# Layer 0's expert call: one token tile's pair weights through GpSimd scatter-adds, and one-hot products for two tiles instead of three

## The chip, the core and the metric

The kernel runs on one core of a Trainium2 chip. The metric is the device time of one execution in microseconds (us); the time quoted for a kernel is the median of its runs. One execution was also taken by the hardware profiler, and all rows below are from that one.

## What is computed

Two layers of attention-like mixers over 256 latent and 256 context tokens, each followed by a PEER expert block, and then a second block of layers. Only the expert block of layer 0 matters here. It works on 512 tokens of width 1024, in four tiles of 128 tokens:

```python
q = (hb @ wq).reshape(tc, PEER_HEADS, 2, PEER_HALF)
s = einsum('thpk,hpnk->thpn', q, keys)            # 8 heads, 2 x 128 keys
s_top, i_top = top_k(s, 16)
cand = s_top[:, :, 0, :, None] + s_top[:, :, 1, None, :]
best, pos = top_k(cand, 16)                       # 16 pairs (i, j) of each head: 128 pairs a token
g = softmax(best)
act = gelu(einsum('td,thed->the', hb, u[eid]))    # eid = 128 * i + j
out = einsum('the,thed->td', g * act, v[eid])
```

There are 128 x 128 = 16384 experts. A token uses at most 128 of them.

## The kernel before

Three of the four tiles (0, 1, 2; together 384 tokens) are computed densely: all 16384 experts are multiplied with all 384 tokens, and a table of weights, zero almost everywhere, picks what counts. The fourth tile (number 3, `SPARSE`) is computed by gathering: for each of its 128 pairs a token, GpSimd fetches the 128 rows of u (`L3484`) and of v (`L3490`), and VectorE makes a dot product (`L3027`) and later a weighted sum (`L3048`).

The dense part has two halves of 128 rounds. A round of the first half ("up") is one block of 128 experts, read from `peer_u` by SyncE's DMA. ScalarE rounds the block to the high part (`L3283`), VectorE makes the low part (`L2925`), both three rounds ahead of use. TensorE multiplies both with the hidden states in 24 products of 384 columns (`L3178` to `L3180`), and ScalarE applies the gelu (`L3290`). A round of the second half ("down") does the same with `peer_v` and the weighted activations (`L3217`). Twelve early up rounds (3, 5, 8, ... 30) also carry a piece of the next layer's modulation.

Beside the up rounds VectorE finds the pairs of each tile ("select"), in the order `TILES = (0, 3, 1, 2)`. How far it goes in a round is a budget in estimated ns: `EARLY_NS` up to the round before the tables begin, then `TABLE_NS` until all four tiles are selected. After this the gathered tile's pieces follow, `PICKS_NS` a round in the up half and `DOWN_NS` a round in the down half; a piece is counted as 1250. The budgets are written into VectorE's program when it is built; they wait for nothing. Within select, ScalarE takes the exponent of the shifted scores (`L3351`, `exp_ready`); its place in ScalarE's queue is the round in which VectorE is planned to have the shifted scores ready (`L2953`), and everything behind it in ScalarE's queue waits with it. The gate of each 8 dot products (`L3323`) stands in ScalarE's queue in the same manner.

A dense tile's pairs are turned by TensorE into `pair_table`: for each token (a column) its 128 values of i, of j and of the share. The table of pair weights then comes four tokens at a time, a group: VectorE compares i and j with 0..127 (`L3058`), ScalarE scales the second by the share (`L3297`, four instructions), TensorE multiplies the two for each token (`L3203`, 8 records for four products), and ScalarE copies the 128 x 512 result (`L3306`). Each four groups SyncE stores a block of 16 tokens, 1 MB, to the DRAM tensor `pair_weights` (`L3469`). 384 tokens are 96 groups and 24 blocks. `TABLE_ROUND` says in which round TensorE does a group, after the 24 products of that round: one group in each round from 32 on, and two in the twelve even rounds 60 to 82, so that the last is in round 115.

GpSimd does nothing in this stage but the gathers: three fetches of u at once, as soon as the spots, the modulation and the first table are ready, then each waits for the dot product that frees its slot. The down half begins by loading the first weights from `pair_weights`.

## Time and profile before

| what | us |
|---|---|
| median of 3 runs (lowest, highest) | 3693.56 (3688.54, 3696.64) |
| the profiled execution, its own time | 3688.0 |
| its span in the trace | 3686.2 |
| up rounds, first to last product | 485.7 to 1175 |
| down rounds | 1183.2 to 1713.5 |
| TensorE busy, share of the span | 3516.4 (95%) |

TensorE is busy for 95% of the span, so what matters is which products it has to do and where it waits. A round is recognised by its 24 products of 384 columns; dividing a stretch by its number of rounds gives the price of a kind of round.

### The profile page before, as it was taken

The numbers are of one execution on the slowest core, as the hardware profiler recorded it, in microseconds if no ns is written. First come the engines' busy times: TensorE is split into PE (matmuls) and PEld (weight loads), VectorE is DVE, ScalarE is ACT, GpSimd is POOL, SyncE is SP. The second block draws the span as 40 slices with busy tenths as digits, with TensorE's granted clock in tenths as the row PEclk, the third lists the DMA queues.
The fourth block names the chain that finished last, engine by engine and source line by source line (L and its number), as shares of the span: only waits on it lengthen the run. The fifth ranks groups of instructions, "written<-read, shape, count | busy, mean of one in ns | idle before, by whom it ended". The sixth has DMA issues, their size and how long they took to land. (4 is left out here: it accounts for less than half of the span.)

```text
span 3686.2 us, 56123 instructions
## 1 busy us (share of the span) xinstructions
PE 3516.4 (95%) x21807; PEld 3143.1 (85%) x21807; DVE 2731.1 (74%) x5467; ACT 1690.3 (46%) x3033; POOL 348.6 (9%) x274
## 2 busy tenths in 40 slices
PE   7999999989999999998999999999997899989899
PEld 6777998989998888887778999988886889988798
DVE  4557379988885888887546987778887677767775
ACT  4343333556663333334543444443334545564554
POOL 0000000014443333330000000000000000000000
PEclk9999999999999999999999999999998999999999
DMA  5133357569998999995124765556664214432143
GB/s 229 71 115 137 138 194 300 173 224 340 371 375 296 333 391 370 377 357 186 56 86 156 233 220 172 169 197 243 242 245 165 98 63 169 186 142 109 69 183 137
DMA packets 184072, 766.75 MB, mean 208 GB/s; under 512 B 23360, under 2 KB 70976, under 8 KB 133888
## 3 DMA queue, kind: packets, MB, share of 16 engines
q1 hardware_dynamic: 146944, 628.92, 47.3%
q0 software_dynamic: 36864, 134.23, 9.4%
q8 instruction: 175, 2.87, 0.3%
q14 instruction: 89, 0.73, 0.1%
HBM read 696.24 MB, written 66.85 MB: 207 GB/s over the span
## 5 line engine op out<-in xcount | busy, mean ns | idle before, releaser
L2925 DVE TENSOR_TENSOR expert_ring_low<-expert_ring,expert_high 128x1024 fp32r<-128x1024 f32 x256 | 312.9, 1222 | 143.5 <-ACT expert_high L3283 137.2
L3283 ACT ACTIVATE expert_high<-expert_ring 128x1024 fp32r<-128x1024 f32 x256 | 270.6, 1057 | 276.2 <-PE ps L3217 264.0
L2192 ACT ACTIVATE expert_high<-expert_ring 128x1024 fp32r<-128x1024 f32 x256 | 270.6, 1057 | 211.3 <-PE ps L2119 211.3
L1922 DVE TENSOR_TENSOR expert_ring_low<-expert_ring,expert_high 128x1024 fp32r<-128x1024 f32 x256 | 311.6, 1219 | 70.7 <-ACT expert_high L2192 70.7
L3178 PE MATMUL ps<-hidden_high,expert_high 128*128 128x384 f32 x1024 | 352.6, 344 | 0.0
L3179 PE MATMUL ps<-hidden_low,expert_high 128*128 128x384 f32 x1024 | 344.4, 336 | 0.0
L3180 PE MATMUL ps<-hidden_high,expert_ring_low 128*128 128x384 f32 x1024 | 344.0, 336 | 0.0
L2088 PE MATMUL ps<-peer_hT_high_peer,expert_high 128*128 128x256 f32 x1024 | 293.9, 287 | 0.6 <-DVE expert_ring_low L1922 0.5
L2089 PE MATMUL ps<-peer_hT_low,expert_high 128*128 128x256 f32 x1024 | 287.0, 280 | 0.0
L2090 PE MATMUL ps<-peer_hT_high_peer,expert_ring_low 128*128 128x256 f32 x1024 | 287.0, 280 | 0.0
L3484 POOL DMA_INDIRECT x<-in_peer_rows,spots x128 | 171.1, 1336 | 971.0 <-ACT mod_next L2378 558.8
L3217 PE MATMUL ps<-expert_high,weighted_high 128*128 128x512 f32 x768 | 237.7, 391 | 9.4 <-DVE weighted_low L3098 9.4
L3217 PE MATMUL ps<-expert_ring_low,weighted_high 128*128 128x512 f32 x768 | 237.0, 390 | 0.0
L3217 PE MATMUL ps<-expert_high,weighted_low 128*128 128x512 f32 x768 | 237.0, 390 | 0.0
L5596 PE MATMUL ps<-hT_high,units_high 128*128 128x256 f32 x704 | 200.2, 284 | 0.0
L5596 PE MATMUL ps<-hT_low,units_high 128*128 128x256 f32 x704 | 199.5, 283 | 0.0
L5596 PE MATMUL ps<-hT_high,weight_ring_low 128*128 128x256 f32 x704 | 199.4, 283 | 0.0
L3490 POOL DMA_INDIRECT chosen_v<-in_peer_v,spots x128 | 171.1, 1336 | 263.2 <-DVE x L3048 246.9
L2088 PEld LDWEIGHTS ps<-peer_hT_high_peer,expert_high 128*128 128x128 f32 x1024 | 194.4, 190 | 1.2 <-DVE expert_ring_low L1922 1.2
L219 DVE TENSOR_TENSOR weight_ring_low<-weight_ring,units_high 128x1024 fp32r<-128x1024 f32 (+1 forms) x148 | 166.9, 1189 | 38.3 <-ACT units_high L210 38.1
L3178 PEld LDWEIGHTS ps<-hidden_high,expert_high 128*128 128x128 f32 x1024 | 194.1, 190 | 0.8 <-issue 0.8
L2089 PEld LDWEIGHTS ps<-peer_hT_low,expert_high 128*128 128x128 f32 x1024 | 194.7, 190 | 0.0
(790 smaller groups left out, 9616.4 us busy)
## 6 DMA issues: line engine op xcount, KB each, us to landing
expert_ring<-in_peer_u SPq DMA_DIRECT2D x128, 1024.0 KB
expert_ring<-in_peer_v SPq DMA_DIRECT2D x128, 1024.0 KB
weight_ring<-in_ffn_w_up SPq DMA_DIRECT2D x22, 2048.0 KB, 7.3
weight_ring<-in_w_in SPq DMA_DIRECT2D x14, 2048.0 KB, 7.8
weight_ring<-in_w_mod SPq DMA_DIRECT2D x12, 2048.0 KB, 8.6
mod_slot<-in_w_mod SPq DMA_DIRECT2D x12, 2048.0 KB, 10.4
pair_weights<-pair_weights_out SPq DMA_DIRECT2D x24, 1024.0 KB
pair_weights_in<-pair_weights SPq DMA_DIRECT2D x15, 1536.0 KB, 15.6
```

Source lines behind the costliest of these rows:

```text
L1922: dve.tensor_tensor(piece(low, n), piece(raw, n), high[:, n % LEAD, :].bitcast(F32), ALU.subtract).then_inc(low_done, 1)
L2088: pe.matmul(o, b[:, s], hT_h[:, c, :], start=(c == 0), stop=False)
L2089: pe.matmul(o, b[:, s], hT_l[:, c, :], start=False, stop=False)
L2090: mm = pe.matmul(o, lo[:, s], hT_h[:, c, :], start=False, stop=(c == DC - 1))
L2192: act.activation(high[:, n % LEAD, :], piece(raw, n), ACT.Identity).then_inc(high_done, 1)
L2925: dve.tensor_tensor(self.piece(G.e_low, n), self.piece(G.e_raw, n), G.e_high[:, n % LEAD, :].bitcast(F32), ALU.subtract).then_inc(self.S.l ...
L3178: pe.matmul(o, b[:, s], B.hs[0][:, c, 0:DW], start=(c == 0), stop=False)
L3179: pe.matmul(o, b[:, s], B.hs[1][:, c, 0:DW], start=False, stop=False)
L3180: mm = pe.matmul(o, lo[:, s], B.hs[0][:, c, 0:DW], start=False, stop=(c == DC - 1))
L3217: mm = pe.matmul(G.ps[:, 2 * t + h, :], (B.ah, B.al)[x][:, r % 3, t * P:(t + 1) * P], v[y][:, h * 512:(h + 1) * 512], start=(r == 0 and (x ...
L3283: act.activation(G.e_high[:, n % LEAD, :], self.piece(G.e_raw, n), ACT.Identity).then_inc(S.high_done, 1)
L5596: mm = pe.matmul(G.ps[:, k % 8, 0:SEQ], w[x][:, c, q * P:(q + 1) * P], self.hT[y][:, c, :], start=(c == 0 and (x, y) == PASSES[0]), stop=( ...
```

## The change

The first tile (0, now `STREWN`) leaves the one-hot products. Its places in `pair_weights` are computed by VectorE (`own_spots`), and GpSimd adds its shares there: 128 indirect DMAs with `compute_op=ADD`, each of 128 single numbers. The eight blocks of this tile are cleared beforehand by eight copies of 1 MB from a constant of zeros, issued by SyncE in the mixer stage long before. Since two heads of a token can have the same pair, GpSimd waits after each 16 scatters (one head) until they have landed. The first 96 scatters come before the first gather; the other 32 are woven with the gathers, one behind each.

The one-hot products are left for 256 tokens, 64 groups and 16 blocks: one group a round in rounds 48 to 111, none doubled. The budgets change. The first fetches of u now wait for the table of tile 1, since tile 0 has none.

```diff
-TABLES_AT = 32
-TABLES = DW // TOKS
+TABLES_AT = 48
+TABLES = (DW - P) // TOKS
-EARLY_NS, TABLE_NS, PICKS_NS, DOWN_NS = 3900, 3300, 2200, 1450
+EARLY_NS, TABLE_NS, PICKS_NS, DOWN_NS = 3200, 3000, 2300, 1500
-DOUBLED = range(60, 84, 2)
-TABLE_ROUND = [r for r in range(TABLES_AT, N_KEYS) for _ in range(2 if r in DOUBLED else 1)][0:TABLES]
+STREWN = 0
+STREWN_FIRST = 6 * PEER_TOPK
+OWN_BLOCKS = P // BLOCK
+TABLE_ROUND = range(TABLES_AT, TABLES_AT + TABLES)
@@ the mixer stage, SyncE
                     ws.run_ahead(sp, u0 + 6)
+                    for b in range(OWN_BLOCKS):
+                        sp.dma_start(G.w_dram[b], G.d["zeros"]).then_inc(G.cleared, 16)
                     sp.wait_ge(S.roped, 6)
@@ select, VectorE
+            elif tile == STREWN:
+                dve.wait_ge(S.base_landed, 16)
+                dve.tensor_scalar(B.own_spots[:, :], B.where[:, :], float(BLOCK), B.base[:, 0:1], ALU.mult,
+                                  ALU.add).then_inc(S.own_ready, 1)
@@ SyncE, before the down half's first weights are loaded
-                sp.wait_ge(S.table_ready, DT)
+                sp.wait_ge(S.table_ready, DT - 1)
+                sp.wait_ge(G.strewn, 16 * PAIRS)
@@ GpSimd
+    def strew(self, pool, m):
+        G, B = self.G, self.B
+        places = G.w_dram.rearrange("b p (n o) -> (b p n) o", o=1)
+        if m and m % PEER_TOPK == 0:
+            pool.wait_ge(G.strewn, 16 * m)
+        pool.indirect_dma_start(places, bass.IndirectOffsetOnAxis(B.own_spots[:, m:m + 1], 0), B.own_share[:, m:m + 1],
+                                None, compute_op=ALU.add).then_inc(G.strewn, 16)
 
     def run(self, pool):
         G, S, B = self.G, self.S, self.B
+        pool.wait_ge(G.cleared, 16 * OWN_BLOCKS)
+        pool.wait_ge(S.own_ready, 2)
+        for m in range(STREWN_FIRST):
+            self.strew(pool, m)
         pool.wait_ge(S.spots_ready, 1)
         pool.wait_ge(S.mod_out, 1)
         pool.wait_ge(S.table_ready, 1)
...
+            if STREWN_FIRST + n < PAIRS:
+                self.strew(pool, STREWN_FIRST + n)
```

On TensorE, the end of round 60 before, where two groups of products (x8 as the program counts them) stand behind the round's last products:

```order
L3179 MATMUL ps<-hidden_low_3340,expert_high 128x384
L3180 MATMUL ps<-hidden_high_3339,expert_ring_low 128x384
L3203 MATMUL ps<-hot_weighted_4886,equal_4885 128x128 x8
L3178 MATMUL ps<-hidden_high_3339,expert_high 128x384
L3179 MATMUL ps<-hidden_low_3340,expert_high 128x384
```

The same place now:

```order
L3189 MATMUL ps<-hidden_low_3348,expert_high 128x384
L3190 MATMUL ps<-hidden_high_3347,expert_ring_low 128x384
L3213 MATMUL ps<-hot_weighted_4894,equal_4893 128x128 x4
L3188 MATMUL ps<-hidden_high_3347,expert_high 128x384
L3189 MATMUL ps<-hidden_low_3348,expert_high 128x384
```

One group is left there. Over the whole program the rows with x8 (12 of them) are gone, and of the 72 with x4 64 are left.

On VectorE, before, the round in which the last tile's shifted scores (`best_shift`) are made, with the comparison of a group (`equal`) ahead; this is planned for round 48:

```order
L2925 TENSOR_TENSOR expert_ring_low<-expert_ring,expert_high 128x1024
L3058 TENSOR_TENSOR equal_4885<-iota,pair_table_4911 128x1024
L1754 MAX_INDEX best_pos_4897<-best_4896,top_work_4891 128x8 x4
L2953 TENSOR_TENSOR best_shift_4903<-best_4896 128x128
L2957 TENSOR_SCALAR pos_row_4898<-best_pos_4897 128x128
L2958 CAST pos_f_4899<-best_pos_4897 128x128
L2961 CAST pos_f_4899<-pos_row_4898 128x128
L2964 TENSOR_SCALAR pos_ij_4900<-pos_f_4899 128x128
L2967 SCALAR_TENSOR_TENSOR pos_f_4899<-pos_ij_4900 128x128
L2970 SCALAR_TENSOR_TENSOR pos_ij_4900<-pos_f_4899 128x128
L2974 TENSOR_TENSOR one_hot_4901<-pos_ij_4900,iota 128x2048
L2925 TENSOR_TENSOR expert_ring_low<-expert_ring,expert_high 128x1024
```

The same place now, planned for round 54:

```order
L2929 TENSOR_TENSOR expert_ring_low<-expert_ring,expert_high 128x1024
L3068 TENSOR_TENSOR equal_4893<-iota,pair_table_4919 128x1024
L1752 MAX best_4904<-top_work_4899 128x8 x4
L1756 MAX_INDEX best_pos_4905<-best_4904,top_work_4899 128x8 x4
L2957 TENSOR_TENSOR best_shift_4911<-best_4904 128x128
L2961 TENSOR_SCALAR pos_row_4906<-best_pos_4905 128x128
L2962 CAST pos_f_4907<-best_pos_4905 128x128
L2965 CAST pos_f_4907<-pos_row_4906 128x128
L2968 TENSOR_SCALAR pos_ij_4908<-pos_f_4907 128x128
L2971 SCALAR_TENSOR_TENSOR pos_f_4907<-pos_ij_4908 128x128
L2929 TENSOR_TENSOR expert_ring_low<-expert_ring,expert_high 128x1024
```

A round holds less of select than before, and the comparison stands in it as before. Select as a whole ends in round 61 instead of 54, and the eighth dot product of the gathered tile, which the first gate waits for, is planned for round 65 instead of 58.

On GpSimd, before, the stage's queue from its start (the first ten fetches of u, then u and v in turn):

```order
L3601 UNCONDITIONAL_BRANCH
L3484 DMA x<-in_peer_rows,spots_4913 128x1024 x10
L3490 DMA chosen_v_4882<-in_peer_v,spots_4913 128x1024
L3484 DMA x<-in_peer_rows,spots_4913 128x1024
L3490 DMA chosen_v_4882<-in_peer_v,spots_4913 128x1024
```

Now, first the start and then, behind the dots, the place where v begins:

```order
L3630 UNCONDITIONAL_BRANCH
L3492 DMA pair_weights<-own_shares_4921,own_spots_4920 6291456x1 x96
L3508 DMA x<-in_peer_rows,spots_4923 128x1024
L3492 DMA pair_weights<-own_shares_4921,own_spots_4920 6291456x1
...
L3508 DMA x<-in_peer_rows,spots_4923 128x1024
L3514 DMA chosen_v_4890<-in_peer_v,spots_4923 128x1024
L3492 DMA pair_weights<-own_shares_4921,own_spots_4920 6291456x1
L3508 DMA x<-in_peer_rows,spots_4923 128x1024
```

96 scatters stand ahead of the first fetch, and one behind each of the first 32 fetches of u.

## Rows read from the trace of the kernel before

**Rows 1.** The page: span and busy time, and the two DMA queues that carry data

```profile
span 3686.2 us, 56123 instructions
PE 3516.4 (95%) x21807; PEld 3143.1 (85%) x21807; DVE 2731.1 (74%) x5467; ACT 1690.3 (46%) x3033; POOL 348.6 (9%) x274
...
q0 software_dynamic: 36864, 134.23, 9.4%
```

**Rows 2.** Windows: stretch and length, then busy us (count) by engine, clock, DMA share, GB/s

```profile
485.70:658.80 173.10, 173.10 (x1096) 153.06 (x1095) 153.79 (x597) 60.44 (x85) 2.56 (x2) 1.00 0.71 261
658.80:1125.60 466.80, 447.79 (x2793) 443.79 (x2791) 409.48 (x645) 286.09 (x661) 160.24 (x111) 0.98 0.83 303
894.00:958.80 64.80, 62.58 (x403) 61.44 (x402) 55.40 (x60) 44.41 (x110) 29.32 (x20) 1.00 0.94 338
984.10:1125.60 141.50, 141.50 (x900) 141.50 (x898) 123.89 (x133) 86.75 (x200) 70.70 (x50) 1.00 0.98 377
1125.60:1171.50 45.90, 45.90 (x267) 45.90 (x267) 24.21 (x25) 16.19 (x23) 15.87 (x11) 1.00 0.80 308
...
1183.20:1713.50 530.30, 528.31 (x2336) 437.15 (x2336) 452.74 (x601) 198.62 (x271) 163.44 (x133) 1.00 0.95 348
```

**Rows 3.** Waits of TensorE between 658.8 and 1125.6: total us, times, longest

```profile
PE ps L3203 <- ACT hot_weighted L3297: 13.1, 6, 5.7
...
PE ps L3203 <- ACT pair_weights_out L3306: 5.7, 9, 2.5
```

**Rows 4.** Timeline around 757: start, duration, engine, line, what; idle before and releaser

```profile
750.99 1.22 DVE L2925 TENSOR_TENSOR expert_ring_low<-expert_ring,expert_high 128x1024 fp32r<-128x1024 f32 x1
...
757.30 1.21 DVE L2925 TENSOR_TENSOR expert_ring_low<-expert_ring,expert_high 128x1024 fp32r<-128x1024 f32 x1
...
760.76 0.29 DVE L2953 TENSOR_TENSOR best_shift<-best 128x128 f32<-128x128 f32 x1
...
761.09 0.31 ACT L3351 ACTIVATE best_exp<-best_shift 128x128 f32<-128x128 f32 x1 [5.13 <-DVE best_shift L2953]
...
765.06 2.04 PE L3203 MATMUL ps<-hot_weighted,equal 128*128 128x128 f32 x8 [5.67 <-ACT hot_weighted L3297]
```

**Rows 5.** Timeline of the first gathers and of the first gate

```profile
655.88 1.17 POOL L3484 DMA_INDIRECT x<-in_peer_rows,spots  x1 [558.80 <-ACT mod_next L2378]
...
795.53 1.68 POOL L3484 DMA_INDIRECT x<-in_peer_rows,spots  x1 [135.54 <-DVE x L3027]
...
803.89 1.89 POOL L3484 DMA_INDIRECT x<-in_peer_rows,spots  x1 [1.74 <-DVE x L3027]
...
816.65 1.22 DVE L3027 SCALAR_TENSOR_TENSOR x<-x,hidden_rows 128x1024 f32<-128x1024 f32 x1 [4.07 <-DMA x<-in_peer_rows,spots]
...
820.56 0.21 ACT L3323 ACTIVATE acts<-dots 128x8 f32<-128x8 f32 x1 [8.72 <-DVE x L3027]
```

**Rows 6.** Groups between 485.7 and 1176: busy us, mean ns, idle before and releasers

```profile
L3297 ACT ACTIVATE hot_weighted<-equal,pair_table 128x128 f32<-128x128 f32 x384 | 122.2, 391 | 64.5 <-DVE equal L3058 64.5
L3058 DVE TENSOR_TENSOR equal<-iota,pair_table 128x1024 f32<-128x1024 f32 x96 | 115.8, 1218 | 0.0
...
L3484 POOL DMA_INDIRECT x<-in_peer_rows,spots x66 | 96.4, 1461 | 794.7 <-ACT mod_next L2378 558.8 <-DVE x L3027 226.4 <-issue 9.5
```

**Rows 7.** The fetches of u by line (min/median/max ns), and the last share of tile 0

```profile
L3484 POOL DMA_INDIRECT x<-in_peer_rows,spots x128: 933/1019/1982, 655.9 to 1627.5; - x128
...
558.40 0.29 DVE L3001 TENSOR_TENSOR selected<-best_exp,best_sum 128x128 f32<-128x128 f32 x1
```

**Rows 8.** SyncE's queue in the mixer stage, first use of the mask, and traffic there

```profile
115.16 0.33 SPq L1693 DMA_DIRECT2D scan_mask<-in_scan_mask  x1
152.68 0.33 SPq L172 DMA_DIRECT2D weight_ring<-in_w_mod  x1
...
L1176 DVE SCALAR_TENSOR_TENSOR mlstm_d<-ps,gcol,scan_mask x32: 475/617/753, 244.8 to 305.5; 128x256 f32<-128x256 f32 x16, 128x512 f32<-128x512 f32 x16
...
112.00:152.00 40.00, 40.00 (x189) 28.09 (x188) 22.01 (x52) 17.12 (x35) 0.00 (x0) 1.00 0.22 86
```

More of the change, by code:

```diff
@@ L55 @@
 SCOPES = []
-STAGE_SEMS = 27
+STAGE_SEMS = 26
 BIG_SEMS = 88
@@ L97, in stage @@
         loads_landed = own[-1]
-        assert len(names) + (3 if beside is not None else 0) < len(own)
+        assert len(names) + (3 if beside is not None else 0) + (1 if loads else 0) <= len(own)
         @block.sync
@@ L2982, in select @@
                 yield 2200
-            if dense >= 2:
-                dve.wait_ge(S.sel_turned, dense - 1)
             for which in range(2):
@@ L2991, in select @@
             step(dve.tensor_reduce(B.sm[:, :, 0], B.ex[:, :, :], AX.X, ALU.add))
-            if tile == SPARSE:
+            if tile in (SPARSE, STREWN):
                 step(dve.scalar_tensor_tensor(B.where[:, :], sel[:, 0, :], float(N_KEYS), sel[:, 1, :], ALU.mult, ALU.add))
@@ L2997, in select @@
                 dve.tensor_copy(B.spots[:, :], B.where[:, :]).then_inc(S.spots_ready, 1)
+            elif tile == STREWN:
+                dve.wait_ge(S.base_landed, 16)
+                dve.tensor_scalar(B.own_spots[:, :], B.where[:, :], float(BLOCK), B.base[:, 0:1], ALU.mult,
+                                  ALU.add).then_inc(S.own_ready, 1)
             yield 600
             step.wait()
-            share = (B.share[:, :] if tile == SPARSE else sel[:, 2, :]).rearrange("p (h m) -> p h m", h=PEER_HEADS)
+            share = {SPARSE: B.share[:, :], STREWN: B.own_share[:, :]}.get(tile, sel[:, 2, :]).rearrange("p (h m) -> p h m", h=PEER_HEADS)
             mm = dve.tensor_tensor(share, B.ex[:, :, :], B.sm[:, :, 1:2].broadcast_to([P, PEER_HEADS, 16]), ALU.mult)
@@ L3003, in select @@
                 step(mm)
+                yield 300
+                continue
+            if tile == STREWN:
+                mm.then_inc(S.own_ready, 1)
                 yield 300
@@ L3058, in equal @@
         dve.tensor_tensor(B.eq[:, g % 2, :, :, :], G.iota[:, :].unsqueeze(1).unsqueeze(1).broadcast_to([P, 2, TOKS, P]),
-                          B.table[:, 0:2, g * TOKS:(g + 1) * TOKS].unsqueeze(3).broadcast_to([P, 2, TOKS, P]),
+                          B.table[:, 0:2, P + g * TOKS:P + (g + 1) * TOKS].unsqueeze(3).broadcast_to([P, 2, TOKS, P]),
                           ALU.is_equal).then_inc(S.eq_ready, 1)
@@ L3184, in turn_selected @@
         G, S, B = self.G, self.S, self.B
-        k = [n for n, t in enumerate(TILES) if t != SPARSE][d]
+        k = [n for n, t in enumerate(TILES) if t not in (SPARSE, STREWN)][d]
         pe.wait_ge(S.sel_ready, d + 1)
@@ L3250, in run @@
                 pe.wait_ge(S.score_s, SCORE_GROUPS // 2)
-            for d in range(DT):
+            for d in range(DT - 1):
                 if r == at[f"turn{d}"]:
@@ L3295, in shares @@
         for k in range(TOKS):
-            t = g * TOKS + k
+            t = P + g * TOKS + k
             act.activation(B.hot_w[:, g % 2, k, :], B.eq[:, g % 2, 1, k, :], ACT.Identity,
@@ L3405, in run @@
         G, S, B, mod = self.G, self.S, self.B, self.mod
+        sp.dma_start(B.base[:, :], G.d["pair_base"]).then_inc(S.base_landed, 16)
         mod.load(sp, 0, self.mod_landed)
@@ L3421, in run @@
                     mod.load(sp, u + 2, self.mod_landed)
-            while stored < BLOCKS and TABLE_ROUND[4 * stored + 3] + 2 <= UJ * p + 1:
+            while stored < BLOCKS - OWN_BLOCKS and TABLE_ROUND[4 * stored + 3] + 2 <= UJ * p + 1:
                 self.store_w(sp, stored)
@@ L3559, in first_experts @@
     B.ge_kept = room(96, 24).take("gelu_kept", [P, STAY - RING, DW], F32)
+    few = room(138, 1.8125)
     B.table = room(127.5, 4.5).take("pair_table", [P, 3, DW], F32)
+    B.own_spots = room(127.5, 0.5).take("own_spots", [P, PAIRS], U32)
+    B.own_share = room(129, 0.5).take("own_shares", [P, PAIRS], F32)
     B.ge_out = room(132, 6).take("gelu_out", [P, 4, DW], F32)
-    few = room(138, 1.8125)
     B.spots = few.take("spots", [P, PAIRS], U32)
@@ L3582, in first_experts @@
     F.ln_cols = few.take("ln_cols", [P, 2, DC], F32)
+    B.base = few.take("own_base", [P, 1], F32)
     B.x_last = F.x_last = room(28.25, 4).take("x_last", [P, D], F32)
@@ L5961, in make_shared @@
     G.v_landed = [nc.alloc_semaphore(f"chosen_v{s}_landed") for s in range(V_SLOTS)]
+    G.w_dram = nc.dram_tensor("pair_weights", [BLOCKS, P, N_KEYS * BLOCK], F32).ap()
+    G.cleared = nc.alloc_semaphore("pair_weights_cleared")
+    G.strewn = nc.alloc_semaphore("shares_strewn")
     G.e_turn = 0
@@ L6098, in constants @@
     f = np.float32
-    c = {"ident": np.eye(P, dtype=f), "pick": np.tile(np.eye(PAD, dtype=f)[:, 0:2], (P // PAD, 1)), "iota": np.tile(np.arange(P, dtype=f), (P, 1))}
+    p = np.arange(P)
+    base = (p // BLOCK * N_KEYS * N_KEYS * BLOCK + p % BLOCK).astype(f)[:, None]
+    c = {"zeros": np.zeros((P, N_KEYS * BLOCK), f), "pair_base": base, "ident": np.eye(P, dtype=f), "pick": np.tile(np.eye(PAD, dtype=f)[:, 0:2], (P // PAD, 1)), "iota": np.tile(np.arange(P, dtype=f), (P, 1))}
     m = np.full((P, 2, QK_WIDTH), NEG, f)
```

10 lines of the change are left out of this document (5 added, 5 removed).

## The prediction

> **What bounds the kernel now.** I read the page first: TensorE is busy for 95% of the span [rows 1], so time can be won only where its products get fewer or its waits shorter. Then the windows of the expert stage [rows 2], because every round has the same 24 products and a stretch divided by its rounds gives a price. Rounds without a group (116 to 126): 45.9 / 11 = 4.17 us. Rounds with one group (88 to 115): 141.5 / 28 = 5.05, so a group costs TensorE 0.88. Rounds 72 to 82 hold six doubled and five single ones: (64.8 - 5 x 5.05) / 6 = 6.59, so the second group of a round costs 1.54, not 0.88. In all three stretches TensorE has no idle time to speak of, and its clock was granted at 1.00, the level of 2.4 GHz.
>
> The whole stretch from round 32 to 115 took 466.8 us for 84 rounds and 12 doublings [rows 2]. By these prices it would be 84 x 5.05 + 12 x 1.54 = 442.7. The rest, 24.1, is stalls. The waits of TensorE there are almost all at the one-hot products: 13.1 us for ScalarE's scaled one-hots, 5.7 for its copies out [rows 3]. The timeline shows where the longest comes from [rows 4]: VectorE needs 757.30 - 750.99 = 6.3 us for a round that TensorE does in 5.05. It is late with the shifted scores, ScalarE stands 5.13 us at its exponent with the gelu, the next block and the one-hots queued behind it, and TensorE then waits 5.67. The second place is the first gate [rows 5]: the fetches issued at 803.89 and after are awaited by VectorE for 4.07 us at 816.65, so ScalarE stands 8.72 us at the gate and TensorE waits again.
>
> The down half is TensorE's alone: 530.3 us with 528.3 busy for 128 rounds, 4.14 a round [rows 2].
>
> **The change, part by part.** I count from 658.8 (round 32) to the end of round 127, before: 466.8 + 12 x 4.17 = 516.8 us.
>
> *TensorE's work.* After: 32 rounds without a group (32 to 47, 112 to 127), 64 with one: 32 x 4.17 + 64 x 5.05 = 456.6. That is 516.8 - 456.6 = 60.2 less if nothing stalled any more; of it 36.1 is work (20 fewer rounds with a group x 0.88 = 17.6, 12 doublings x 1.54 = 18.5) and 24.1 is all stalls of before. So the question is which stalls come back.
>
> *Start of the tables.* VectorE does two comparisons in the round before the first group, now round 47. I take 1 us of stall (0 to 2; one of the waits of [rows 3]).
>
> *Fourth exponent, now round 54.* Before, VectorE had table rounds from 32 on ahead of round 48, of 6.3 us at the worst [rows 4] and some 5.9 on average by the budget (3.3 of select plus two instructions of 1.14 net, and the small gaps). In the nine rounds since its last pause it fell behind by about 9 x (5.9 - 5.05) = 7.7 us. Now the budget is 0.3 less, and only seven table rounds stand before round 54: 7 x 0.55 = 3.9, plus 1.1 for the doubled comparison: 5.0. The stall there, about 9 us before with the slower clock after it (the 2.04 us group of [rows 4], against about 1.05 for an undisturbed one), becomes about 9 - 2.7 = 6.5. Bounds: 2 and 9.
>
> *Rounds 32 to 47.* They get shorter for TensorE (4.17), and VectorE with 3.2 of select and one low part is at 4.4 to 4.5: no longer slack as in the modulation rounds (173.1 / 32 = 5.4 each [rows 2]). The third exponent (round 38) and the first turning (44) fall here. ScalarE and VectorE work three rounds ahead, which hides most of it. I take 4 us, bounds 0 and 8.
>
> *First gate, now round 65.* The same start of gathers, with 1.84 dot products a round instead of 1.76 and a scatter between two fetches. I take the stall of before, about 6.5 with its waits of [rows 5], plus 1.5 for one scatter ahead of the late fetch: 8. Bounds 4 and 14.
>
> *Doubled rounds and the block stores.* The copies out that waited (5.7 [rows 3]) belong to them; one group a round leaves eight rounds for two blocks. 0 to 1: I take 0.5, with the second turning.
>
> Sum of stalls: 1 + 6.5 + 4 + 8 + 0.5 = 20. After: 456.6 + 20 = 476.6, against 516.8: **40 us less**.
>
> *VectorE and ScalarE* lose 32 comparisons of 1.22 and 128 scalings of 0.39 [rows 6]; they are not the bound in those rounds, and what this gives is counted above.
>
> *GpSimd's scatters.* No row shows an accumulating DMA. Nearest: a fetch of u, 0.93 to 1.98 us, median 1.02 over the stage, mean 1.46 in the busy up half [rows 6, 7], plus 0.3 from one to the next. I take 1.34, so 1.64 each. Tile 0's shares were ready at 558.4 [rows 7]; with the lower budget some two rounds later, about 570. The 96 take 157 us. The five waits are for a landing: nothing below, and above the 12.8 us from 803.89 to 816.65 [rows 5]; I take 4. End: 570 + 157 + 20 = 747 (697 to 853 with both ends everywhere: 96 x 1.32, or 96 x 2.28 and 64 us of waits). The first dot product comes at about 658.8 + 16 x 4.17 + 4 + 13 x 5.05 + 1 + 6.5 = 803. So 56 us of cover; the three first fetches are issued after the table of tile 1 instead of at 655.88, and are not missed before 803. If the cover is gone, each us is TensorE's: behind the dot product stand the low parts of all further blocks.
>
> The Trainium skill ("DMA: Bandwidth & Descriptors", section "Anatomy of one DMA") gives a fixed cost of about 2.0 us to a DMA from GpSimd. If that held the queue for each scatter, it would be 96 x 2.3 = 221 us, an end at about 811 and an 8 us loss; the fetches of u here, at a median of 1.02 us, hold GpSimd's queue for less.
>
> *The woven 32.* A pair then costs GpSimd 3 x 1.76 = 5.3 us in the busy half, against one pair in 5.05 / 0.92 = 5.5. Just enough; 0, up to 10 if a scatter takes 2.
>
> *Their transfers.* 36864 packets of the gathers' queue took 9.4% of 16 engines [rows 1]: 0.094 x 16 x 3686 / 36864 = 0.15 us a packet of 4 KB. 128 packets of one number: 1.2 us at most of the 16 engines if they cost as much, nothing at the least; I take 0.2. With one group a round the DMA share was 0.98 at 377 GB/s and TensorE did not wait [rows 2]; the picks add 0.04 pairs of 1 MB a round, 8 GB/s. 0, up to 15.
>
> *Clearing.* 8 MB at about 113 us, behind SyncE's last load and ahead of the mask (115.16). The DMA share is 0.22 there [rows 8]. At 377 GB/s it is 22 us, at half that 45: over at about 160. The mask is first used at 244.8, the next load (152.68) later than that. SyncE's eight issues take some 4 us in which it had nothing to do. 0 on the path.
>
> *Down half.* 1500 instead of 1450: VectorE stays at about 3.6 of 4.14 us. It ends with products, unchanged: 0.
>
> The sum stands against the profiled execution: 3688.0 - 40 = 3648. The median of runs lies 5.6 above it; I say **3651**, between the two ways of placing it.
>
> **Rivals.**
> 1. *Slow scatters: slower than before.* Three things of the list above in one mechanism: GpSimd's queue is serial, and the first fetch stands behind 96 scatters. At a price s each (with the gap), the fetches come at 590 + 96 s, and the loss is 96 s - 213, plus 23 (s - 2.0) for the woven ones once v is fetched too. It eats 40 us at s = 2.5. At s = 3.3 the time would be 3688 - 40 + 104 + 30 = 3782. For it: an accumulate has to read before it writes, 128 places each in another row of the memory, and 16 are outstanding at a time where the gathers had three or four. Against: the longest fetch, 512 KB, took 1.98. The skill's same page (section "Specifications") says that transfers under 512 B are done as read-modify-write, which speaks for it; no row here can show what that costs.
> 2. *DMA becomes the bound in rounds 62 to 120.* At 0.98 share and 5.05 a round, a scatter at 1.2 us of all engines would make 5.05 x 0.98 + 0.1 + 1.2 = 6.2 for the 32 rounds or so in which they are woven: half of it late, about 20 us lost: 3670.
> 3. *The stalls are not there.* With smaller budgets VectorE is never late, and the exponent and gate wait cost nothing: 60 instead of 40, 3631.
> 4. *TensorE's groups were hidden anyway*, so that nothing is gained: 3690. Against: no idle time in the stretches of [rows 2].
>
> **How the numbers follow.** What a measurement can tell here is 0.2%, 7.4 us. Chances: forecast, 25 to 52 us less, 0.62; rival 2 and late first fetches, 8 to 25 less, 0.16; rival 3, more than 52, 0.05; within 7.4, 0.05; slower, 0.12. Faster 0.83, same 0.05, slower 0.12. The range: the stall bounds sum to 6 and 32, so 26 to 54 below 3688 to 3693; I leave out rival 1 and half of rival 2: 3637 to 3674.
>
> **What would show it.** A single-group round at 5.05 and an empty one at 4.17; the up half (485.7 to 1175) ending near 1135; the down half still 530. No wait at copies out. ScalarE waiting at the exponent of round 54 and the gate of 65, some 5 us each. Scatters at about 1.3 us on GpSimd, ended before 800. Wrong if scatters take over 2.4, if VectorE waits long at the first dot product, if rounds 62 to 95 are over 5.2, or if the down half grows.

## The result, and the profile after

The changed kernel takes 3673.99 us (median of 4 runs, 3669.64 to 3674.43) against 3693.48 (3688.54 to 3696.64): ratio 0.9946, interval 0.9929 to 0.9963. It is faster, by 19.5 us, just under half of the 40 that were forecast. The profiled execution has a span of 3672.4 against 3686.2.

The page of the changed kernel, the lines that answer to [rows 1]:

```profile
span 3672.4 us, 55502 instructions
...
PE 3492.1 (95%) x21548; PEld 3116.7 (85%) x21548; DVE 2695.5 (73%) x5436; ACT 1638.2 (45%) x2873; POOL 591.6 (16%) x402
...
q0 software_dynamic: 55296, 134.31, 10.6%
```

TensorE's busy time is 24 us less. GpSimd's went from 348.6 to 591.6; the scatters are 249.4. The gathers' queue has 18432 packets more, 144 a scatter (128 with a number each and 16 more, all of 4 bytes), and only 0.1 MB more.

The windows of the changed kernel (columns as in [rows 2]): rounds 0 to 31; 32 to the first dot products; to round 91; nearly 13 rounds with one group; the down half:

```profile
488.20:661.00 172.80, 172.80 (x1093) 152.71 (x1093) 140.61 (x514) 60.66 (x85) 70.64 (x40) 1.00 0.78 260
661.00:826.00 165.00, 156.94 (x932) 155.39 (x931) 148.32 (x432) 80.20 (x154) 123.97 (x67) 0.98 0.68 180
826.00:985.60 159.60, 142.22 (x855) 141.03 (x855) 120.17 (x135) 81.79 (x187) 131.57 (x80) 0.95 0.95 328
1014.00:1079.00 65.00, 65.00 (x414) 65.00 (x413) 58.55 (x64) 40.34 (x93) 34.80 (x25) 1.00 1.01 396
...
1165.00:1696.20 531.20, 527.47 (x2332) 436.36 (x2333) 461.87 (x613) 198.68 (x271) 176.07 (x141) 1.00 0.97 355
```

The fourth row has no idle TensorE, and rounds there take 5.05 us: the price of a round was right. The third row is where the loss is: TensorE idles for 17.4 of 159.6 us, and GpSimd is busy for 131.6; with the 0.30 us that stand between any two of its 80 instructions, 24 us, hardly anything is left. The down half is unchanged (531.2 against 530.3).

The waits of the changed kernel between rounds 32 and 127: what waited, for what, total, times, longest. They answer to [rows 3]:

```profile
DVE x L3037 <- DMA x<-in_peer_rows,spots: 43.3, 16, 8.5
...
ACT acts L3333 <- DVE x L3037: 35.8, 7, 12.6
...
PE ps L3213 <- ACT hot_weighted L3307: 23.8, 7, 8.5
...
POOL pair_weights L3492 <- DMA pair_weights<-own_shares,own_spots: 14.9, 4, 5.9
...
ACT best_exp L3361 <- DVE best_shift L2957: 8.9, 2, 5.1
```

The first three lines are a chain. VectorE waits for a fetched u 16 times; ScalarE stands at the gate for VectorE's dot product with the one-hots queued behind; TensorE then waits for the scaled one-hots. The wait for the copies out [rows 3] is gone, and the exponent's is as long as before (5.1).

The changed kernel's timeline, where GpSimd runs through three pairs, and the first gate with TensorE's wait for it:

```profile
847.50 0.21 ACT L3333 ACTIVATE acts<-dots 128x8 f32<-128x8 f32 x1 [12.56 <-DVE x L3037]
...
849.47 0.77 PE L3213 MATMUL ps<-hot_weighted,equal 128*128 128x128 f32 x2 [8.53 <-ACT hot_weighted L3307]
...
865.79 2.69 POOL L3492 DMA_INDIRECT pair_weights<-own_shares,own_spots  x1 [0.30 <-issue]
868.78 0.97 POOL L3508 DMA_INDIRECT x<-in_peer_rows,spots  x1 [0.30 <-issue]
870.06 0.95 POOL L3514 DMA_INDIRECT chosen_v<-in_peer_v,spots  x1 [0.30 <-issue]
871.32 2.04 POOL L3492 DMA_INDIRECT pair_weights<-own_shares,own_spots  x1 [0.30 <-issue]
873.67 1.39 POOL L3508 DMA_INDIRECT x<-in_peer_rows,spots  x1 [0.31 <-issue]
```

In these three pairs GpSimd waits for nothing but its own queue. From the fetch at 845.79 to that at 904.40 are ten pairs, 5.9 us each, where VectorE's budget wants one in 5.5. And the scatters of the changed kernel, by line (min/median/max ns):

```profile
L3492 POOL DMA_INDIRECT pair_weights<-own_shares,own_spots x128: 1542/1602/4510, 573.2 to 978.7; - x128
```

Their mean is 1.95, not the 1.34 taken; the front ones average 1.87, the woven ones 2.18. Of the waits for a landing five stand among the 96 (19.5 us), one among the woven ones (1.3). The 96th starts at 804.14, and the first fetch follows at 806.10, where 747 was forecast.

### The profile page after: what moved, and what is told of

It is laid out like the page before. It is cut to its first block and busy times, and to the rows that moved or that the text cites. A ratio compares the mean times of both kernels' runs of the same rounds, so it can differ in the third digit from the quotient of the medians.

```text
span 3672.4 us, 55502 instructions
## 1 busy us (share of the span) xinstructions
PE 3492.1 (95%) x21548; PEld 3116.7 (85%) x21548; DVE 2695.5 (73%) x5436; ACT 1638.2 (45%) x2873; POOL 591.6 (16%) x402
## 5 line engine op out<-in xcount | busy, mean ns | idle before, releaser
L2929 DVE TENSOR_TENSOR expert_ring_low<-expert_ring,expert_high 128x1024 fp32r<-128x1024 f32 x256 | 312.7, 1222 | 125.8 <-ACT expert_high L3293 116.5
L3492 POOL DMA_INDIRECT pair_weights<-own_shares,own_spots x128 | 249.4, 1948 | 540.2 <-DVE own_shares L3007 473.7
```

Of the source, the lines that this page charges most:

```text
L2929: dve.tensor_tensor(self.piece(G.e_low, n), self.piece(G.e_raw, n), G.e_high[:, n % LEAD, :].bitcast(F32), ALU.subtract).then_inc(self.S.l ...
```

## The experiments

Theory A: what is short is GpSimd's time. Its queue is serial, and a scatter between two fetches makes the fetches late. Theory B: it is the transfers, 128 packets of 4 bytes a scatter, that hold up the others. Each kernel has the median of 4 to 10 runs, and beside it stands the kernel before on the same chip. The changed kernel (3673.99) had a kernel before at 3693.48 beside it, the others had one at 3687.86 to 3692.43; so a difference between two changed kernels is given by the medians and, where it matters, by the traces, as the time of rounds 32 to 127 (496.6 us in the changed kernel).

**Without any scatter**, and with only the front or only the woven ones. The first also takes out the waits for them:

```diff
-        for m in range(STREWN_FIRST):
-            self.strew(pool, m)
...
-            if STREWN_FIRST + n < PAIRS:
-                self.strew(pool, STREWN_FIRST + n)
```

> The changed kernel without any of the 128 scatters (tile 0's blocks of the table stay zero, so its weights are left out of the result); clearing, budgets and everything else as changed. Theory A, the scatters fill GpSimd's queue so that the fetches come late: the 28 us of stalls between rounds 61 and 95 fall to the 6 to 8 us of a first gate, and the time from 3674 to about 3654. Theory B, the scatters' packets load the DMA engines: the same. Theory C, the stalls come from the shorter budgets and the one-group schedule, not from the scatters: 3670 or more.

> Only the 96 scatters ahead of the first fetch; the 32 woven ones are left out (a quarter of tile 0's shares are missing from the table). Theory A: the first fetch is still issued at about 806, the gate of round 65 still stalls TensorE by about 10, the 16 us of stalls in rounds 74 to 91 go: about 3658. If the first 96 carry the loss: 3670. If the woven ones alone do: 3654.

> Only 32 scatters, one behind each of the first 32 fetches of u; the 96 ahead of the first fetch are left out (three quarters of tile 0's shares are missing). The first fetch comes right after the table of tile 1, at about 725. Theory A: the first gate stalls as before, 6 to 8; GpSimd still has about 5.6 us of work a pair against 5.5, so part of the stalls in rounds 74 to 91 stays: 3658 to 3666. Theory B (traffic) expects the same stalls there as in the changed kernel.

Measured, with the kernel before at 3690.92: none 3652.83 (ratio 0.9894, 0.9877 to 0.9911); front only 3654.25 (0.9900, 0.9883 to 0.9917); woven only 3665.89 (0.9932, 0.9912 to 0.9953). So the 96 front ones, 231 us of GpSimd's time, cost 1.4 us, though they end 59 us later than forecast: the fetches at 806 are still early enough. The 32 woven ones cost 13.1 by themselves, but two of their four executions lie at 3661 and two at 3670, and the profiled one is of the lower two. Together they cost 21.2 in the medians (3673.99 less 3652.83), 18.6 with each taken from its own kernel before, and 20.9 in the traces (rounds 32 to 127: 496.6 less 475.7). So 4 to 7 us are a joint effect. The traces place 7.0 at the first gate: TensorE's stall in rounds 67 to 70 (time of a round above its price) is 7.2 us with none, 5.5 with front only, 6.1 with woven only and 11.4 with both.

**Plain writes instead of accumulating ones**, all 128:

```diff
-                                None, compute_op=ALU.add).then_inc(G.strewn, 16)
+                                None, compute_op=ALU.bypass).then_inc(G.strewn, 16)
```

> All 128 scatters, but as plain writes instead of additions (a pair that two heads of a token share keeps one share only). If the price of a scatter is GpSimd's writing of 128 descriptors, nothing moves: a scatter still holds GpSimd for 1.54 us or more and the time is 3674 within 3. If it is the reading before the write: the landing waits (3 to 6 us each now) shrink and the time goes towards that without scatters, about 3660.

Measured: 3764.52 (1.0195, 1.0162 to 1.0227). A plain scatter holds GpSimd for 0.96 us against 1.54 for an undisturbed accumulating one, so the addition itself costs 0.6. But the kernel is 90 us slower than the changed one, which neither expectation had. Nor is the kind of write all that the edit changes: the gathers' queue now has 4096 packets more than before instead of 18432 (40960 in all), and the trace shows a plain scatter as 16 packets of 32 bytes and 16 of 4. Its page's line of that queue, and its windows from the first scatter on:

```profile
q0 software_dynamic: 40960, 134.31, 9.3%
...
560.00:580.00 20.00, 20.00 (x131) 16.63 (x130) 15.41 (x47) 5.51 (x8) 5.94 (x6) 1.00 0.92 358
...
600.00:640.00 40.00, 11.82 (x29) 5.42 (x24) 6.21 (x28) 2.46 (x4) 28.91 (x30) 0.59 0.14 37
640.00:680.00 40.00, 7.20 (x15) 4.59 (x16) 3.05 (x17) 0.60 (x1) 29.17 (x31) 0.50 0.02 0
...
720.00:760.00 40.00, 40.00 (x253) 34.94 (x252) 36.11 (x92) 14.64 (x20) 0.00 (x0) 1.00 0.79 299
```

and TensorE's timeline in it:

```profile
658.71 0.48 PE L3188 MATMUL ps<-hidden_high,expert_high 128*128 128x384 f32 x1 [2.32 <-issue]
661.51 0.48 PE L3189 MATMUL ps<-hidden_low,expert_high 128*128 128x384 f32 x1 [2.32 <-issue]
```

Every engine but GpSimd all but stops until just after the 96 are through (at 700.7), and the DMA engines are not what they wait for: the DMA share is 0.02, and TensorE waits for nothing that the profile shows, 2.32 us before each product. The granted clock falls to 0.50, the level of 1.2 GHz, after it stopped. This told nothing on A and B yet; it comes back below.

**GpSimd's time without transfers, in two sizes.** Each woven scatter is replaced by a chain of short memsets:

```diff
             if STREWN_FIRST + n < PAIRS:
-                self.strew(pool, STREWN_FIRST + n)
+                for k in range(7):
+                    pool.wait_ge(G.cleared, 16 * OWN_BLOCKS + 7 * n + k)
+                    pool.memset(B.table[0:1, 2, 0:P], 0.0).then_inc(G.cleared, 1)
```

> The changed kernel with 96 scatters in front as they are; each of the 32 woven scatters is replaced by seven short memsets on GpSimd, each waiting for the one before, of 0.2 us by the nearest rows (128x36 takes 0.14, 128x256 0.31), so about 2 us of GpSimd's time a pair and no transfer at all. The last 32 pairs' shares of tile 0 are left out of the table. Theory A (GpSimd's serial queue is what is short: a pair costs it 6.3 us where VectorE takes one in 5.5) expects the loss of the woven scatters to stay: TensorE stalls of some 12 us in rounds 74 to 91 and some 10 at the gate of round 67, a time of 3668 to 3675. Theory B (the scatters' transfers, 128 packets of 4 bytes each, hold up the gathers' and the blocks' transfers) expects the time of the kernel with only the front ones, 3654, and no stall in rounds 74 to 91.

> As the run with seven short memsets in place of each woven scatter, but with ten: 10 x 0.245 + 0.17 = 2.6 us of GpSimd's time a pair instead of 1.9 (a woven scatter of the changed kernel takes 2.18 + 0.30, and its landing waits 0.28 a pair: 2.76), and still no transfer. The last 32 pairs' shares of tile 0 are left out. A pair costs GpSimd then 2 x 1.65 + 2.6 = 5.9 us against VectorE's 5.5. Theory A (GpSimd's time) expects the stalls of rounds 74 to 91 to come back (10 to 15 us) in every execution: 3666 to 3674. Theory B (transfers) expects 3655, as with seven.

Measured: 3655.62 (before 3690.59; 0.9909, 0.9892 to 0.9925) with seven, 3672.29 (before 3687.86; 0.9954, 0.9936 to 0.9972) with ten. GpSimd in the kernel with ten, and what VectorE and TensorE wait for:

```profile
871.91 0.94 POOL L3514 DMA_INDIRECT chosen_v<-in_peer_v,spots  x1 [0.31 <-issue]
872.85 2.46 POOL L3519 MEMSET pair_table<- 1x128 f32 x10
875.48 0.95 POOL L3508 DMA_INDIRECT x<-in_peer_rows,spots  x1 [0.17 <-issue]
...
DVE x L3037 <- DMA x<-in_peer_rows,spots: 35.6, 12, 8.2
...
PE ps L3213 <- ACT hot_weighted L3307: 24.5, 9, 8.9
```

The run with seven met theory B's expectation (3654) and missed A's (3668 to 3675); that run alone would have pointed at the transfers. The size decided it: without one byte moved, 2.6 us of GpSimd's time a pair brings nearly the whole loss back (3672.3; the changed kernel 3674.0; in the traces rounds 32 to 127 take 494.0 of the 496.6), with the same waits in the same places. With 1.9 us three runs of four lie at 3655 and one, the profiled one, at 3663: that is the edge. A woven scatter with its gap is 2.48, so the ten memsets are a little longer than what they stand for; whether the last 2.6 us of the loss are the one landing wait among the woven ones (1.3) or the transfers stays open.

**The transfers without GpSimd's time:** SyncE writes 32 columns of 128 numbers in the same rounds.

```diff
+                for k in (2 * (p - 31), 2 * (p - 31) + 1):
+                    sp.dma_start(B.w_dram[k % OWN_BLOCKS][:, 61 * k:61 * k + 1], B.own_share[:, STREWN_FIRST + k:STREWN_FIRST + k + 1], allow_slow_non_contiguous=True).then_inc(
+                        G.cleared, 16)
```

> The transfers without GpSimd's time: the 96 front scatters as they are; in place of the 32 woven ones SyncE writes 32 columns of 128 numbers (4 bytes each, 8 KB apart) into the table, two behind each page of two rounds from round 62 to 94, so that in the same rounds as many 4-byte packets go to DRAM as the scatters send, but GpSimd's queue is free of them. The last 32 pairs' shares land in places of no meaning, without addition. If GpSimd's time is the whole cause: the time with only the front ones, 3654 to 3657, and stalls of at most 4 us in rounds 74 to 91. If the transfers have a part of their own (the run with plain woven writes lay 10 us above the one with seven memsets at about the same GpSimd time): 3660 to 3666.

Measured: 3653.97 (before 3692.43; 0.9897, 0.9880 to 0.9913), the time with only the front ones. B falls for the packets as such: these are 144 a write as with a scatter (4608 more in SyncE's queue), between 823.7 and 979.3, and they cost nothing. What they do not stand for is the addition and GpSimd's queue. An accumulating scatter's packets take longer, 27 ns at the median against 9, so that a scatter costs 0.31 us of the 16 DMA engines and a write of SyncE 0.08. But the traces do not show that this slows the fetches. With the gathers' 4 KB packets counted off in the order of GpSimd's queue, gathers 10 to 66 of the changed kernel end 7.1 us after their issue (10.2 at most), and 8.1 us (11.0) in the kernel without scatters. The latter also stand closer together, so this is no price of a scatter; but the fetches of the changed kernel are issued late and do not travel longer.

**Shorter scatters: plain woven ones, and all for 16 tokens.**

```diff
-                                None, compute_op=ALU.add).then_inc(G.strewn, 16)
+                                None, compute_op=ALU.add if m < STREWN_FIRST else ALU.bypass).then_inc(G.strewn, 16)
@@ the other kernel
-        ... bass.IndirectOffsetOnAxis(B.own_spots[:, m:m + 1], 0), B.own_share[:, m:m + 1],
+        ... bass.IndirectOffsetOnAxis(B.own_spots[0:16, m:m + 1], 0), B.own_share[0:16, m:m + 1],
```

> The changed kernel with the 96 front scatters accumulating as they are and the 32 woven ones as plain writes (no addition, so a pair that two heads share keeps one of its shares). The count and the size of the transfers stay; a plain write takes GpSimd 0.96 us instead of 1.6 or more, so a pair costs it 2 x 1.7 + 1.3 = 4.7 us. Theory A expects the stalls of rounds 74 to 91 to go from 15 to 4 or less: 3656 to 3662. Theory B expects no difference from the changed kernel, 3670 to 3674. The stall of 112 us that the kernel with all writes plain had in rounds 18 to 20 should not come, if it is from 96 plain writes issued 1.26 us apart.

> The changed kernel with each of its 128 scatters made for tokens 0 to 15 of tile 0 alone (16 numbers instead of 128); the other tokens' shares are left out. This prices a scatter by its length. If GpSimd's time is fixed by the instruction (1.54 us at least, 1.95 on average, as with 128), Theory A expects the time of the changed kernel, 3670 to 3674, and Theory B 3654 to 3658, since an eighth of the transfers is left. If GpSimd's time goes with the number of places (0.5 us or less for 16), the 96 end at about 660 and both expect 3653 to 3657; then this run tells only the price.

Measured, before at 3687.86: plain woven 3666.04 (0.9941, 0.9921 to 0.9961), 4 us above A's range; 16 tokens 3662.93 (0.9925, 0.9906 to 0.9944), between the two. A scatter of 16 numbers holds GpSimd for 1.28 us undisturbed, one of 128 for 1.54: the price is nearly fixed, 0.26 us for 112 numbers. Neither run separates A from B, the first less so as it also changes the packets (16 of 32 bytes in place of 128 of 4; its expectation had their count and size unchanged). Plain woven ones (1.37 + 0.30 a pair) lie 10 us above the seven memsets (1.9) in the medians, though the two profiled executions have the same span, 3661.6, since that of the memsets was its slowest; why plain ones are over the edge more often stays open.

**No landing waits:** a table of its own for each head.

```diff
-        places = G.w_dram.rearrange("b p (n o) -> (b p n) o", o=1)
-        if m and m % PEER_TOPK == 0:
-            pool.wait_ge(G.strewn, 16 * m)
+        places = (G.w_dram if m < PEER_TOPK else G.apart[m // PEER_TOPK - 1]).rearrange("b p (n o) -> (b p n) o", o=1)
```

> The changed kernel with a table of its own in DRAM for each of the 8 heads' scatters, so that GpSimd never waits for a landing (six waits, 20.8 us in the changed kernel); only head 0's shares reach the table that the down half reads. The 96 scatters should end at about 785 instead of 806. Theory A expects the gate stall of round 67 to shrink from 9.6 to 5, since the first three fetches come some 20 us before the first dot product, and the stalls of rounds 74 to 91 to shrink by the waits that stood there, 3 of the 13 us: 3662 to 3668. If the gate stall came from the woven scatters alone, it stays at 9 and the time is 3669 to 3673.

Measured: 3664.80 (before 3690.59; 0.9936, 0.9919 to 0.9952). The first fetch comes at 782.3, and the stall of rounds 67 and 68 goes from 11.4 to 6.7. Rounds 32 to 127 take 487.3 us, 9.3 less than in the changed kernel: 4.7 of it stands at the gate and 3.6 in rounds 70 to 91. That is again GpSimd's time, 20.8 us of waits in the changed kernel. In the medians, each against its own kernel before, it is 6.3. The edit also spreads the shares over eight tables, so the two are shown together.

**The clearing alone,** in the kernel before:

```diff
                     ws.run_ahead(sp, u0 + 6)
+                    for b in range(8):
+                        sp.dma_start(G.w_dram[b], G.d["zeros"]).then_inc(G.cleared, 16)
```

> The kernel before with the clearing alone: eight copies of 1 MB of zeros into the table in the mixer stage, and SyncE waiting for them ahead of the expert stage. Expected by both theories: no difference from before (within 0.1%), 3690. If the clearing delays the mixer stage's loads, a longer mixer stage and up to 10 us more.

Measured: 3692.38 against 3690.59, ratio 1.0003 (0.9993 to 1.0013): nothing, as taken.

**A better place for the scatters.** Two behind each three pairs, from pair 8 on; then the same with select's budget moved to the front:

```diff
-            if STREWN_FIRST + n < PAIRS:
-                self.strew(pool, STREWN_FIRST + n)
+            if n >= 8 and n % 3 != 1 and STREWN_FIRST + (2 * (n - 8) + 1) // 3 < PAIRS:
+                self.strew(pool, STREWN_FIRST + (2 * (n - 8) + 1) // 3)
@@ the second kernel also
-            return EARLY_NS if r < TABLES_AT - 1 else TABLE_NS
+            return 3900 if r < 31 else 2800 if r < TABLES_AT - 1 else 2500
```

> The changed kernel, all 128 scatters kept and 96 in front, but the woven 32 stand behind two of each three pairs from pair 8 on (pairs 8 to 54) instead of behind each of the pairs 0 to 31. GpSimd then needs 2 x 1.76 + 2/3 x 2.25 = 5.0 us a pair, less than VectorE's 5.5, and the first gate has no woven scatter ahead of its fetches. Theory A expects nearly the time without any scatter: gate stall back to about 4, rounds 74 to 91 with at most 4 us of stalls instead of 13, 3654 to 3660. Theory B (each scatter's transfer costs the gathers something wherever it stands) expects the same total as the changed kernel less at most the gate, 3664 to 3672.

> The version with two scatters behind each three pairs from pair 8 on, and with other budgets for select: 3900 a round in rounds 0 to 30, 2800 in rounds 31 to 46, 2500 after, instead of 3200 and 3000. Tile 0's shares are then ready about 14 us earlier, the 96 scatters end at about 792 instead of 806, select ends three rounds earlier than in the changed kernel and the first dot product stands in round 62 instead of 61. Expected: the exponent's stall (5.7 + 1.9 in rounds 56 and 57) smaller, since VectorE has less of select in a table round, and the gate's stall (6.0 + 0.8) down to 4, since the first fetches come 14 us ahead of their use: 3648 to 3655 against 3657.7. Rival: both stalls stay, because VectorE is then late in rounds 0 to 31 instead, 3657 to 3662.

Measured: 3657.67 (before 3690.59; 0.9916, 0.9899 to 0.9932) and **3646.01** (before 3687.86; 0.9881, 0.9865 to 0.9897). All 128 scatters are in both. The second beats the kernel before by 42 us and the changed one by 22 to 28 (22 with each against its own kernel before, 28 in the profiled spans). Its windows of rounds 32 to 127, and its waits of TensorE there:

```profile
663.00:1130.60 467.60, 461.61 (x2824) 460.20 (x2822) 389.92 (x602) 250.30 (x525) 334.30 (x207) 0.99 0.90 317
...
PE ps L3213 <- ACT hot_weighted L3307: 5.9, 3, 4.4
```

Rounds 0 to 31 take no longer, with VectorE busy for 161 instead of 141 us of them; the exponent's stall (7.6 us in rounds 56 and 57) is gone. What is left is a stall of 7.5 in rounds 64 and 65. The budgets' part was worth a little more than expected (3648 to 3655).

**The stop of all engines.** All scatters plain, but the front ones spaced by three memsets; and all plain with 16 numbers:

```diff
         for m in range(STREWN_FIRST):
+            for k in range(3):
+                pool.wait_ge(G.cleared, 16 * OWN_BLOCKS + 3 * m + k)
+                pool.memset(B.table[0:1, 2, 0:P], 0.0).then_inc(G.cleared, 1)
             self.strew(pool, m)
```

> All 128 scatters as plain writes (no addition), but each of the 96 front ones behind three short memsets in a chain (0.73 us), so that they are issued about 2.0 us apart instead of 1.26. If the stall of 112 us in rounds 18 to 20 came from the density of plain writes, it is gone: 3656 to 3664, with the first fetch at about 765. If it comes from plain 4-byte writes as such, however they are spaced, a stall of some 100 us or more stays: 3760 or over.

> All 128 scatters as plain writes, each for tokens 0 to 15 alone (16 numbers); the other tokens' shares are left out. They should be issued 1.0 us apart or less (an accumulating one of 16 took GpSimd 1.28 us, one of 128 took 1.54, a plain one of 128 took 0.96). If the 112 us stall comes from the number of 4-byte writes in a us (100 with 128 numbers each 1.26 us; 69 with the accumulating ones, which did not stall; here some 16), it is gone: 3652 to 3660. If it comes from the number of plain indirect DMAs in a us, it stays or grows: 3760 or over.

Measured, before at 3692.43: spaced 3661.12 (0.9912, 0.9896 to 0.9929), no stop; 16 numbers 3771.44 (1.0217, 1.0200 to 1.0234), the stop is there. So neither plain writes as such nor the count of numbers stops the engines. What the two stopped kernels share, and the spaced one lacks, is indirect DMAs 1.26 and 1.15 us apart. It is not the count of packets either: 32 a scatter in both, against 144 each 1.85 us in the changed kernel, which does not stop. Accumulating scatters never stood closer than 1.58 us, so what they would do at 1.2 is not known.

**All in one view.** The windows of rounds 70 to 91, 22 rounds with one group, 111.1 us at 5.05. The changed kernel:

```profile
863.02:989.84 126.82, 116.04 (x707) 114.84 (x706) 99.34 (x108) 67.95 (x156) 106.34 (x65) 0.97 0.98 347
```

The same of the kernel without scatters:

```profile
857.17:969.01 111.84, 111.84 (x706) 111.84 (x706) 101.55 (x109) 68.34 (x158) 61.28 (x42) 0.99 0.99 378
```

With seven memsets (its longest execution):

```profile
859.08:976.67 117.59, 113.56 (x707) 112.98 (x706) 98.09 (x107) 68.24 (x158) 89.84 (x176) 0.99 0.99 371
```

With ten memsets:

```profile
864.00:987.84 123.84, 114.76 (x707) 113.31 (x706) 101.37 (x109) 68.72 (x158) 98.01 (x246) 0.99 0.95 359
```

With SyncE's writes:

```profile
856.19:967.65 111.46, 111.46 (x706) 111.29 (x706) 102.75 (x111) 69.15 (x160) 62.75 (x42) 1.00 1.02 395
```

The last version, with early budgets:

```profile
851.13:962.86 111.73, 111.60 (x706) 111.31 (x706) 103.41 (x113) 68.91 (x160) 92.16 (x55) 1.00 1.02 388
```

The DMA share says nothing here (0.95 to 1.02 in all). GpSimd's busy time (106.34, 61.28, 89.84, 98.01, 62.75, 92.16) with 0.30 a gap fills the stretch in the changed kernel: 106.3 + 65 x 0.3 = 125.8 of 126.8. Where gaps are of several sizes, as with the memsets, its waits tell it better: the time for which GpSimd waits in the stretch for another engine (a slot that VectorE has still to free) or for a landing. With ten memsets it is 3.3 us, in four waits for VectorE. For all kernels, beside what the stretch takes above 111.1:

| kernel | GpSimd waits, us | stall, us |
|---|---|---|
| changed | 1.3 | 15.7 |
| woven scatters only | 3.4 | 13.1 |
| scatters of 16 numbers | 3.9 | 13.8 |
| no landing waits | 1.9 | 12.1 |
| ten memsets | 3.3 | 12.7 |
| plain woven scatters | 8.4 | 7.4 |
| all plain, the front spaced | 10.1 | 7.3 |
| seven memsets (its longest execution) | 9.9 | 6.5 |
| two of three, old budgets | 8.2 | 5.1 |
| two of three, early budgets | 6.5 | 0.6 |
| SyncE's writes | 41.1 | 0.4 |
| front scatters only | 42.0 | 0.1 |
| no scatters | 43.8 | 0.7 |

Every kernel that stalls has a queue that is full or nearly so, whether scatters or memsets fill it. The last version is the exception: its queue is at 92.2 + 55 x 0.3 = 108.7 of 111.7 and it stalls nowhere. It is not that every third fetch has no scatter ahead, since the version with the old budgets has that too and stalls for 5.1. With the early budgets the first fetch is issued at 786.1 instead of 805.8, so the queue may enter the stretch without arrears. This last step is argued, not shown: no run starts the fetches earlier and changes nothing else.

## Why the prediction was half right

**TensorE's work and the stalls without scatters: right.** The forecast for rounds 32 to 127 was 456.6 + 20 = 476.6 us. The kernel without scatters took 1132.56 + 4.17 - 661.08 = 475.7, and 38.1 less than before in the medians where 40 were forecast. Term by term (stalls above 5.05 or 4.17 in the changed kernel): start of tables 1.3 (1 taken); exponent 7.6 in rounds 56 and 57 (6.5); rounds 32 to 47 2.3 (4); doubled rounds 0; gate, without scatters, 7.2 (8). The clearing and the down half cost nothing, as said.

**What failed** is the step "The woven 32 ... Just enough; 0, up to 10 if a scatter takes 2". It measured 13.1 alone and, with the gate, about 20 together (15.7 us of stalls in rounds 70 to 91, where the sum had none). A woven scatter takes 2.18 us, not 1.46, so a pair costs GpSimd 2 x 1.64 + 2.48 = 5.8 us, not 5.3 (5.9 by the ten pairs above; the 0.28 of landing waits a pair that one expectation counts was a mistake, they stand in front). I had compared 5.3 with 5.5 and called it enough: at 96% of a serial queue's time a small error in one price turns cover into the bound. The range's upper end (3674) came by another way, from half of rival 2's DMA; that the measurement (3673.99) lies on it is luck. Rival 1 had the right term: its 23 (s - 2.0) for the woven ones gives 11 at the measured s of 2.48. The stall bounds, too, were added wrongly: they sum to 6 and 34, not 32; the 26 that follows is what 34 gives.

**The price of a scatter** "I take 1.34" measured 1.87 in front. At the front this did no harm: the queue ran 59 us later than forecast, all of the "56 us of cover" was used, and it cost 1.4. Besides the price, five waits of 3.9 on average (4 taken) and one pause of 6.4 that the profile puts down to issue stand in it. The rest of rival 1 (96 s - 213 with s = 2.17 would be nothing) was right. The rule of the Trainium skill that I weighed ("DMA: Bandwidth & Descriptors", section "Anatomy of one DMA", about 2.0 us for a DMA from GpSimd, an end at 811) was nearer than my row of 1.02: the end was 806. The nearness is chance, for it is not that figure that holds the queue: plain scatters hold it for 0.96, accumulating ones for 1.54.

**The gate** "plus 1.5 for one scatter ahead of the late fetch" was short when the front ran up to it: the gate measured 11.4 where 8 were taken, and 5.5 to 7.2 without the front, the woven ones or both. Between the first eight fetches stand seven scatters, not one.

**Rival 2** (transfers) is refuted in its size: as many packets from SyncE cost nothing, and a scatter took 0.31 us of all DMA engines (0.2 taken, 1.2 in the rival). Rival 3 was wrong for these budgets, but the last version shows what it was worth: with less of select in the table rounds the exponent's stall does go.

## What to carry to other kernels

When work is given to an idle engine, add up its time per unit of the loop that it shares by measured prices, gaps and all, and leave room: here 5.2 us of GpSimd in 5.5 cost 1 us in the median (9 in one execution of four), 5.9 cost 18. A replacement that only spends time, and one that only moves bytes, tell a full queue from full DMA engines, if the first is tried in more than one size: seven memsets alone would have misled. Place such work where nobody waits behind it (here ahead of the first fetch: 96 scatters for 1.4 us), and spread the rest.

## What the runs showed of the hardware

- An indirect DMA's hold on GpSimd's queue hardly depends on its length: undisturbed, accumulating 1.54 us for 128 numbers and 1.28 for 16; plain 0.96 and 0.84; 0.30 more to the next. Beside other work single ones take about 1 us longer (0.95 and 1.95, 1.6 and 2.6). In the changed kernel's up half, 54 of GpSimd's DMAs overlap none of VectorE's instructions of over 1.1 us (low parts, comparisons, dot products, weighted sums and a few of select), and not one of them took 0.1 us more than undisturbed; of the 189 that overlap one, 123 took over 0.3 us more. The Trainium skill ("DMA: Bandwidth & Descriptors", section "SWDGE vs HWDGE vs iDMA") says that GpSimd writes the descriptors into SBUF, and that VectorE locks it out there while it runs in its 2-port mode. The trace agrees in so far as the extra time stands only beside long VectorE instructions; it does not show the mode that they ran in, and no run took them away.
- An accumulating scatter of 128 numbers is 144 packets of 4 bytes, at 27 ns the median; a plain one is 16 of 32 bytes and 16 of 4. Each accumulating one took 0.31 us of the 16 DMA engines.
- 96 indirect DMAs issued 1.26 or 1.15 us apart (plain; of 128 and of 16 numbers) stopped the other engines: rounds 0 to 31 took 112 and 119 us longer. With 128 numbers single products stood 2.8 us apart, with a DMA share of 0.02 and the clock at 0.50. At 1.58 us (accumulating, 16 numbers) and at 1.83 and 1.85 (plain and spaced; accumulating) nothing of this is seen. What is starved was not found. "issue", the wait that the profile gives, fits instructions that come late to the engines; the packets of the trace's instruction queues took 1.03 us at most in the first stop, against 1.20 in the changed kernel between 540 and 730, and none came between 602.5 and 715.0, which may as well follow from engines that do nothing.
